# Moving the index heads of a sparse-attention layer one input slab forward, on one Trainium2 core

## What is computed

```python
proj = h @ w_in
qc, kc, vc, qi, ki, wi, cq, ckv, kr = _split(proj, ODD_SIZES)   # qi: 8 heads x 32, ki: 32, wi: 8
...
rel = relu(einsum("bqhe,bse->bqhs", qi, ki) * D_IDX ** -0.5)
score = einsum("bqhs,bqh->bqs", rel, wi * N_IDX ** -0.5)
score = where(causal, score, -inf)
_, idx = lax.top_k(score, topk)                                 # topk = 128
```

## Time and profile before

| | us |
|---|---|
| median of 3 runs | 1243.86 (1242.53 to 1245.54) |
| the profiled execution | 1239.07 |
| its span in the trace | 1237.2 |
| PE busy | 1190.9 (96% of the span) |
| DVE busy | 679.0 (55%) |
| ACT busy | 511.0 (41%) |
| POOL busy | 532.6 (43%) |

### The profile page before, as it was taken

How to read it: one execution, slowest core, us unless ns; L and a number is a source line. 1 busy time by engine, 2 the same in 40 slices (tenths; PEclk the granted TensorE clock), 3 DMA queues, 4 the chain that set the end, 5 groups by cost and what they waited for, 6 DMA issues and landing times. The chain is left out here.

```text
span 1237.2 us, 15976 instructions
## 1 busy us (share of the span) xinstructions
PE 1190.9 (96%) x5705; PEld 984.1 (80%) x5709; DVE 679.0 (55%) x1041; ACT 511.0 (41%) x914; POOL 532.6 (43%) x286
## 2 busy tenths in 40 slices
PE   7999997999999999999999798999999999999997
PEld 5688886878888888888777687888788888888886
DVE  5766675665144153165568999646651541632654
ACT  6677575433222222224354377763322222322333
POOL 2443432434444444447623465434344444444441
PEclk9999998999999999999999999999999999999998
DMA  5222221333333333333322101102333333333332
GB/s 158 71 68 73 65 69 35 93 86 102 102 87 101 102 90 97 102 92 94 87 67 69 52 1 35 35 19 71 92 92 102 99 90 101 101 88 99 102 90 80
DMA packets 188922, 100.83 MB, mean 82 GB/s; under 512 B 8806, under 2 KB 186257, under 8 KB 188866
## 3 DMA queue, kind: packets, MB, share of 16 engines
q1 hardware_dynamic: 187596, 99.97, 28.2%
q10 hardware_dynamic: 1270, 0.13, 0.1%
HBM read 97.92 MB, written 2.16 MB: 81 GB/s over the span
## 5 line engine op out<-in xcount | busy, mean ns | idle before, releaser
L1550 POOL TENSOR_TENSOR wl<-raw,wh 128x1024 fp32r<-128x1024 f32 x172 | 420.6, 2446 | 566.1 <-ACT wh L1120 566.1
L665 PE MATMUL bank<-ur,wh 128*128 128x512 f32 x1080 | 422.0, 391 | 0.2 <-POOL wl L1550 0.2
L666 PE MATMUL bank<-ur,wh 128*128 128x512 f32 x1080 | 420.6, 389 | 0.0
L667 PE MATMUL bank<-ur,wl 128*128 128x512 f32 x1080 | 420.4, 389 | 0.0
L1120 ACT ACTIVATE wh<-raw 128x1024 fp32r<-128x1024 f32 x172 | 181.7, 1058 | 520.6 <-PE bank L667 520.5
L665 PEld LDWEIGHTS bank<-ur,wh 128*128 128x128 f32 x1080 | 203.1, 188 | 42.8 <-issue 1.1
L666 PEld LDWEIGHTS bank<-ur,wh 128*128 128x128 f32 x1080 | 203.1, 188 | 42.4 <-issue 0.5
L667 PEld LDWEIGHTS bank<-ur,wl 128*128 128x128 f32 x1080 | 203.0, 188 | 42.2
L1880 DVE TENSOR_TENSOR xT<-bank,xT 128x512 f32<-128x512 f32 x64 | 44.2, 691 | 227.7 <-PE bank L667 227.5
L1713 DVE TENSOR_TENSOR ur<-sq,ur 128x512 fp32r<-128x512 f32 x65 | 129.8, 1998 | 45.5 <-ACT ur L1120 45.5
L665 PE MATMUL bank<-xh,wh 128*128 128x512 f32 (+1 forms) x296 | 120.8, 408 | 3.9 <-DVE xl L1776 3.9
(11 more groups left out here) (217 smaller groups left out, 1355.3 us busy)
## 6 DMA issues: line engine op xcount, KB each, us to landing
raw<-in_w_mlp SPq DMA_DIRECT2D x128, 512.0 KB, 3.8
raw<-in_w_in_e SPq DMA_DIRECT2D x18, 512.0 KB, 3.6
raw<-in_w_in_o SPq DMA_DIRECT2D x10, 512.0 KB, 3.7
raw<-in_w_out_e SPq DMA_DIRECT2D x8, 512.0 KB, 3.8
raw<-in_w_out_o SPq DMA_DIRECT2D x8, 512.0 KB, 3.7
strip_raw<-bias_rows SPq DMA_DIRECT2D x8, 256.0 KB, 3.1
out<-probs SPq DMA_DIRECT2D x4, 512.0 KB, 2.6
probs<-in_x SPq DMA_DIRECT2D x2, 512.0 KB, 4.3
```

The costliest lines, as they stand in the source:

```text
L665: mm(dst, lhs[0], rhs[0], start=start, stop=False, skip_group_check=not check)
L666: mm(dst, lhs[0], rhs[1], start=False, stop=False, skip_group_check=not check)
L667: return mm(dst, lhs[1], rhs[0], start=False, stop=stop, skip_group_check=not check)
L1550: return nc.gpsimd.tensor_tensor(dst, a, b, ALU.subtract)
```

## The change

Six things change, all in layer 1's input projection, and nothing else in the program.

1. PE runs only tiles 0 to 2 of slab 2 before the index heads. The other tiles of slab 2 and tiles 0 to 6 of slab 3 stand between the heads (table `IDX_TILES`: 2, 2, 1, 3, 1, 1, 1, 1), and slabs 4 and 5 come whole behind them.
2. The low halves of the index key and the index queries are made by POOL (`split_key_index`, `split_query_index`). The key's is made for 32 partitions and copied to the other 96 by ACT (`ki_spread`).
3. DVE clears `score` ahead of the norm, POOL puts the causal mask into it, and all eight heads are added to that.
4. DVE takes slab 2 and ACT rounds `qi1` just ahead of head 3's relu (`QI1_HEAD`).
5. ACT splits slab 3 behind head 0's relu and slab 4 behind head 3's; `cq0` and `cq1` are handled by ACT and DVE behind the heads.
6. `ROUNDS_AT` gets a round after slab 3 and one after slab 4, so that 10 of 16 rounds, not 8, stand ahead of the head steps.

```diff
-ROUNDS_AT = (0, 0, 0, 0, 0, 1, 2, 1, 2, 1, 1)
+ROUNDS_AT = (0, 0, 0, 1, 1, 1, 2, 1, 2, 1, 1)
+IDX_TILES = (((2, 3), (2, 4)), ((2, 5), (2, 6)), ((2, 7),), ((3, 0), (3, 1), (3, 2)), ((3, 3),), ((3, 4),), ((3, 5),), ((3, 6),))
+QI1_HEAD = 3
...
 # tensor
-            input_slab(2)
-            input_slab(3)
+            slab_tiles(N_IN1 + 2, range(3), range(KT))
             pe.wait_ge(wi_scaled, 1)
...
-            pe.wait_ge(p_lo, SPLIT0 + 3)
             for i in range(N_IDX):
+                if i == 0:
+                    pe.wait_ge(ki_lo, 1)
+                if i == 1:
+                    pe.wait_ge(ki_spread, 1)
+                if i % 4 == 0:
+                    pe.wait_ge(qi_lo, i // 4 + 1)
...
-                slab_tiles(n, [2 * (i % 4), 2 * (i % 4) + 1], range(KT))
+                for m, k in IDX_TILES[i]:
+                    slab_tiles(N_IN1 + m, [k], range(KT))
+            slab_tiles(N_IN1 + 3, [KT - 1], range(KT))
+            input_slab(4)
+            input_slab(5)
...
 # scalar, of slab 0
+                    copy(ki[0][0:32, :], t[0:32, :]).then_inc(p_hi, 1)
                     copy(w_scaled, t[32:32 + N_IDX, :], float(N_IDX ** -0.5)).then_inc(wi_scaled, 1)
-                    for r in range(0, P, 32):
-                        last = copy(ki[0][r:r + 32, :], t[0:32, :])
-                    last.then_inc(p_hi, 1)
+                    for r in range(32, P, 32):
+                        copy(ki[0][r:r + 32, :], t[0:32, :])
...
 # scalar
             split_slab(N_IN1 + 2)
-            split_slab(N_IN1 + 3)
             projected(p0, "nar", N_IN1)
             projected(p0 + 1, "qi0", N_IN1 + 1)
-            split_slab(N_IN1 + 4)
-            projected(p0 + 2, "qi1", N_IN1 + 2)
-            split_slab(N_IN1 + 5)
-            projected(p0 + 3, "cq0", N_IN1 + 3)
+            act.wait_ge(ki_lo, 1)
+            for r in range(32, P, 32):
+                last = copy(ki[1][r:r + 32, :], f32(ki[1][0:32, :]))
+            last.then_inc(ki_spread, 1)
...
 # gpsimd
+            def cut_future():
+                pool.wait_ge(score_clear, 1)
...
+            def split_key_index():
+                pool.wait_ge(p_hi, SPLIT0 + 1)
+                sub(ki[1][0:32, :], tbuf[0:32, N_IN1 % 2, :], ki[0][0:32, :].bitcast(F32)).then_inc(ki_lo, 1)
+            def split_query_index(i):
+                pool.wait_ge(p_hi, SPLIT0 + i + 2)
+                sub(qi[1][:, i, :], tbuf[:, (N_IN1 + i + 1) % 2, :], qi[0][:, i, :].bitcast(F32)).then_inc(qi_lo, 1)
...
 # vector
+            v.memset(score[:, :], 0.0).then_inc(score_clear, 1)
             rsqrt("mix_o", rstd[:, :])
...
+                if i in (3, 4):
+                    projected(p0 + i, ODD[i][0], n)
```

More of the change, by code:

```diff
@@ L337, in trunk @@
         idx_added = sem("idx_added")
+        score_clear = sem("score_clear")
         causal_cut = sem("causal_cut")
+        ki_lo = sem("ki_lo")
+        ki_spread = sem("ki_spread")
+        qi_lo = sem("qi_lo")
         mask_ready = sem("mask_ready")
@@ L1475, in _ @@
             split_slab(N_IN1 + 2)
-            split_slab(N_IN1 + 3)
             projected(p0, "nar", N_IN1)
             projected(p0 + 1, "qi0", N_IN1 + 1)
-            split_slab(N_IN1 + 4)
-            projected(p0 + 2, "qi1", N_IN1 + 2)
-            split_slab(N_IN1 + 5)
-            projected(p0 + 3, "cq0", N_IN1 + 3)
+            act.wait_ge(ki_lo, 1)
+            for r in range(32, P, 32):
+                last = copy(ki[1][r:r + 32, :], f32(ki[1][0:32, :]))
+            last.then_inc(ki_spread, 1)
             for i in range(N_IDX):
+                if i == QI1_HEAD:
+                    projected(p0 + 2, "qi1", N_IN1 + 2)
                 for blk in (1, 2, 3):
@@ L1492, in _ @@
                                          scale=float(D_IDX ** -0.5)).then_inc(relu_ready, 1)
-                if i == 5:
-                    split_slab(N_IN1 + 6)
-                    projected(p0 + 4, "cq1", N_IN1 + 4)
+                if i == 0:
+                    split_slab(N_IN1 + 3)
+                if i == QI1_HEAD:
+                    split_slab(N_IN1 + 4)
             act.wait_ge(kr_rotated, 2)
@@ L1507, in _ @@
             steps = head_steps(2 * NH, 4 * NH)
-            for i in range(5, len(ODD)):
+            for i in range(3, len(ODD)):
                 n = N_IN1 + i
+                if i in (4, 5):
+                    projected(p0 + i - 1, ODD[i - 1][0], n - 1)
                 if i == 6:
@@ L1657, in output_lo @@
                 sub(att(1, tile), o_f32(j), att(0, tile).bitcast(F32)).then_inc(att_lo, 1)
+            def cut_future():
+                pool.wait_ge(score_clear, 1)
+                for blk in (1, 2, 3):
+                    c0 = SC[blk][0] + P * blk
+                    last = nc.gpsimd.affine_select(out=score[:, c0:c0 + P], in_=score[:, c0:c0 + P], compare_op=ALU.is_ge,
+                                                   fill=NEG, base=0, pattern=[[-1, P]], channel_multiplier=1)
+                last.then_inc(causal_cut, 1)
+            def split_key_index():
[4 more added lines that the diff above has]
+                sub(qi[1][:, i, :], tbuf[:, (N_IN1 + i + 1) % 2, :], qi[0][:, i, :].bitcast(F32)).then_inc(qi_lo, 1)
             for n in range(LEAD):
@@ L1675, in _ @@
             mlp(N_MLP0, GROUPS - 1)
-            for n in range(N_IN1 - 2 * KT, N_IN1 + 7):
+            for n in range(N_IN1 - 2 * KT, N_IN1 + 3):
                 split(n % 2, n)
@@ L1680, in _ @@
                     low(m)
[L1682 to L1687, removed]
+                if n == N_IN1 + 1:
+                    cut_future()
+            split_key_index()
+            split_query_index(0)
+            split((N_IN1 + 3) % 2, N_IN1 + 3)
+            split_query_index(1)
+            for n in range(N_IN1 + 4, N_IN1 + 7):
+                split(n % 2, n)
             steps = head_steps(2 * NH, 4 * NH)
@@ L1758, in take_slab @@
                 dve.wait_ge(slab_done, n + 1)
-                if n >= N_IN1 and dst is None:
-                    dve.wait_ge(p_lo, SPLIT0 + n - N_IN1 - 1)
-                elif n >= 2 and n - 2 != FA and dst is None:
+                if n in (N_IN1 + 2, N_IN1 + 3, N_IN1 + 4) and dst is None:
+                    dve.wait_ge(p_hi, SPLIT0 + n - N_IN1 - 1)
+                    if n == N_IN1 + 2:
+                        dve.wait_ge(ki_lo, 1)
+                        dve.wait_ge(ki_spread, 1)
+                    else:
+                        dve.wait_ge(qi_lo, n - N_IN1 - 2)
+                elif n >= N_IN1 + 2 and dst is None:
+                    dve.wait_ge(p_lo, SPLIT0 + n - N_IN1 - 4)
+                elif 2 <= n < N_OUT0 and n - 2 != FA and dst is None:
                     dve.wait_ge(p_lo, placed(n - 2))
@@ L1810, in projected @@
                             last = sub(kb[1][HD * d:HD * (d + 1), kv, :], t[rows, :], kb[0][rows, kv, :])
-                elif name == "nar":
-                    for r in range(0, P, 32):
-                        last = sub(ki[1][r:r + 32, :], t[0:32, :], ki[0][0:32, :])
                 elif name == "kv":
@@ L2078, in _ @@
             rotate(tbuf[:, N_IN1 % 2, :])
[L2079 to L2083, removed]
+            take_slab(N_IN1 + 1)
             dve.wait_ge(wi_turned, 1)
@@ L2087, in _ @@
             dve.wait_ge(low_lo, N_LOW)
-            projected(p0 + 3, "cq0", N_IN1 + 3)
+            dve.wait_ge(causal_cut, 1)
             for i in range(N_IDX):
+                if i == QI1_HEAD:
+                    take_slab(N_IN1 + 2)
                 for blk in (1, 2, 3):
@@ L2092, in _ @@
                     dve.wait_ge(relu_ready, 3 * i + blk)
[L2093 to L2096, removed]
+                    if i:
                         dve.wait_ge(idx_added, 3 * (i - 1) + blk)
[L2098 to L2104, removed]
+                    v.scalar_tensor_tensor(score[:, c0:c0 + w], relu[:, c0:c0 + w], widx[:, blk, i:i + 1],
+                                           score[:, c0:c0 + w], ALU.mult, ALU.add).then_inc(idx_added, 1)
+            dve.wait_ge(idx_added, 3 * N_IDX)
             dve.wait_ge(kr_hi, 1)
@@ L2108, in _ @@
             last.then_inc(kr_ready, 1)
-            dve.wait_ge(causal_cut, 1)
             def latent_values_lo(a):
```

15 lines of the change are left out of this document (7 added, 8 removed).

## The result

The changed kernel takes 1253.88 us (median of 4, 1250.80 to 1255.64), the kernel before beside it 1243.22 (4, 1242.53 to 1245.54). The ratio is 1.0093, 95% interval 1.0065 to 1.0122: slower by 10.7 us, where +2.0 was forecast and 1249.5 was the upper end of the range. The profiled execution is 1250.80 with a span of 1248.9, 11.7 over the span before.

A forecast was written before the change was run, and what follows sets the result against it. DVE was taken to set PE's pace from 665 to about 770, its taking of slab 5 being the mark. 3.6 us later there, less 1.6 given back, put +2.0 on 1243.86: 1245.9 us, range 1240.5 to 1249.5.

The forecast's parts named there:

- Start of the index heads: Ahead of head 0: POOL's subtraction collides with DVE's rotary key; head 0 starts at 625.0 after PE waits 2.9 us.
- The clock: Behind the wait ahead of head 0: lower clock in heads 0 and 1 loses 1.5 us; bounds nothing and 3.6.
- Through the heads: Index heads: 2.67 us with one tile, 4.05 with three; DVE's last add at 651.25, 9.3 us earlier.
- From there to slab 5: DVE's chain from last add to taking slab 5: 14.8 us, so slab 5 at 666.05, 3.6 us later.
- What the later stretch gives back: Head steps behind slab 5: steps 20 and 21 lose rounds, the mask comes earlier; net 1.6 us back.
- Sum: Whole kernel: 3.6 - 1.6 = +2.0 us, put on the median 1243.86 for 1245.9.
- D: Slower rival, 0.22: wait ahead of head 0 costs 3.6 us of clock, adds held up about 1 us; 1249.0.
- B: Rival, 0.20: no collision and no loss of clock at the start of the index heads; 1243.4, no change.
- C: Faster rival, 0.18: as B, and DVE early enough that PE's waits at 754.51 and 756.52 go; about 1240.

The follow-up runs named there:

- the combined kernel: Changed kernel with short wait, two tiles behind every head, slab 3 taken among the heads; 1239.81 us with both moved rounds, 1239.39 with none, 1234.51 with one.

## The prediction against the runs

**Start of the index heads: right.** Forecast head 0 at 625.0 behind a wait of 2.9 us; measured 625.19 and 3.02, for POOL, and the clock fell about 2 us later. The collision was there: 1.82 us for the key's low half, 2.38 for the rotary key's last two operations (1.40 in the earlier trace rows). The Trainium skill has this rule in "SBUF — State Buffer", section Who interferes with whom: a DVE operation with two SBUF inputs contends with a GpSimd operation that reads SBUF, and the contention is an exclusive lock. The trace agrees with 2.38 us for 1.40 and 1.82 for the 1.29 of the earlier trace rows. The same section says that `tensor_scalar` can contend as well; the 3.02 us for 0.87 of the four small ones agree.

**The clock, and through the heads: this is where it failed.** "The clock" charged 1.5 us behind the wait, and heads 0 and 1 took 8.19 us, 1.5 lost: right in itself. But the step took it that the clock answers to waits alone, and "Through the heads" then priced one-tile heads at 2.67 us from matmuls at full clock. The last add ended at 661.39, not 651.25: 10.1 us, lost at 0.50 with PE busy. Two tiles a head took the long fall away, one tile a head brought it to the kernel before, and 128 rows took it away with the tiles unchanged. I had even the row that could have warned: the heads' matmuls were known as 32 rows high, and one tile in place of two halves the full-height work between them.

The Trainium skill, "TensorE: Matmul & The Clock Gate", section What's actually happening, says that the gate goes by how busy PE has been of late. The runs differ from it, if busy is what the profile counts as busy: PE was busy for 26 of 26 us at 0.50 with 32 rows, and had 1.00 with 128 rows at the same order of matmuls.

**From there to slab 5: nearly right.** 15.7 us from last add to slab 5 in place of 14.8. The 0.9 is the low half of `cq0` behind POOL's split (1.58 in place of 0.75), and some of the sum of squares (1.18; the 0.8 of the sum stands in no row). With the 10.1 of the heads and the 3.6 forecast that makes 14.6.

**What the later stretch gives back: right.** The lag of 14.6 is passed on nearly as it is, 14.1 at 730.90, 14.3 at 778.47, and falls to 12.5 at 785.14, so 2.1 us come back in all, 1.8 of them at the mask (forecast 1.6). The forecast read 1.9 us of wait from its row; 764.14 + 2.50 is 766.64, and the row itself has 1.56. The mask at 766.88 stands ahead of the low halves as foreseen, and makes PE's wait there 2.19 us:

```profile
766.88 0.73 DVE L2037 TENSOR_SCALAR mask_c<-score 128x1152 bf16<-128x1152 f32 x1
```

**Sum.** 2.0 forecast; 10.1 of clock in the heads and 0.9 of DVE's chain on top give 13.0, less 0.5 that came back beyond the forecast, 12.5. That is still the lag at PE's last wait, 2.26 us in both (1224.54 and 1237.06). Behind it the kernel before ran at the lower clock in the recorded execution (its 8 small matmuls took 1.84 us, and 1.06 after), which takes 0.8 off: 11.7 by the spans. In the second execution of the kernel before they took 1.02. That last step is luck of the recorded executions and no effect of the change.

**Rivals.** D had the right side and the right resource, and the wrong place: it charged a wait of over about 3 us with 3.6 us of clock; the wait was 3.02, and that fall cost 1.5. B and C are refuted in what they supposed (no collision; DVE early enough), though the combined kernel shows that C's direction was to be had with other tile counts. The range failed because its upper bound for the clock was taken from a wait, and no bound was set for PE running a mix of matmuls that the kernel before did not have. Even for the mix that it had, one execution was a poor price: 1.5 us in the one, 6.1 in the other.

## What to carry to other kernels

Where matmuls that use part of the array's rows are interleaved with full ones, as here, treat the share of full ones as a resource: spreading them thinner put a busy PE at 1.2 GHz for nearly as long as the mix lasted, and a busy share of 100% does not show it; read the granted clock of the stretch. When work is moved on DVE or POOL by a few microseconds, look at which instruction of the other engine it now meets: the same four operations were 0.87 or 3.02 us. Place moved work by what each piece removes; one round removed the mask's wait and filled time in which DVE waited, the second made the chain ahead of slab 5 longer and brought the four operations into POOL's split.

## What the runs showed of the hardware

The granted clock depended on the rows used and not on the busy time alone: 0.50 through 26 us of full busy time with 32-row matmuls and one tile a head, 1.00 in the same window with 128 rows, and 1.00 with two tiles a head in the four combined executions. Two tiles a head did not always bring a fallen clock back soon: behind the same wait of 1.04 us the heads stood at 0.50 for about 3 us in one execution and for over 12 in another. Equal waits of 1.56 us cost a fall in one execution and none in the next. What stays open is why the short wait ahead of one-tile heads regained more than the wait itself, whether the rows of the matmuls or of their weight loads count, and what decides with two tiles and one in turn, where executions of one kernel took 1240.33 to 1249.05 us.
